# Moving the three operations of each unit that form the imaginary part of its second table from DVE to GpSimd

## What is computed

```
    lam_dt = lam * dt[:, None]
    lam_bar = jnp.exp(lam_dt)
    b_bar = ((lam_bar - 1.0) / lam)[..., None] * bmat
    powers = jnp.exp(lam_dt[None] * jnp.arange(1, S5_CHUNK + 1, ...)[:, None, None])
    ...
        _, xs = lax.associative_scan(_ssm_combine, (a, bu), axis=1)
        xs = xs + powers[None] * h[:, None]
        y = jnp.einsum('btgp,gsp->btgs', xs, cmat).real
```

## Time and profile before

| | |
|---|---|
| median of 3 runs | 1574.27 us (1570.85 to 1575.98) |
| span of the profiled execution, first to last instruction | 1571.2 us |
| PE busy | 1503.4 us, 96% |
| DVE busy | 872.9 us, 56% |
| ACT busy | 402.3 us, 26% |
| POOL busy | 565.2 us, 36% |
| share of PE in the chain that ended last | 88% |

### The profile page before, as it was taken

One profiled execution on the slowest core, in us unless ns is written; L12 is line 12 of the kernel. 1 busy time (PEld: TensorE's weight loads), 2 busy tenths in 40 slices (PEclk: granted clock), 3 DMA queues, 4 the chain that ended last, 5 costly groups with the idle time before them and its releaser, 6 DMA issues.

```text
span 1571.2 us, 25477 instructions
## 1 busy us (share of the span) xinstructions
PE 1503.4 (96%) x10192; PEld 1129.3 (72%) x10192; DVE 872.9 (56%) x1745; ACT 402.3 (26%) x956; POOL 565.2 (36%) x412
## 2 busy tenths in 40 slices
PE   4999989999999999999998999999999999999998
PEld 3455555666655558898877888887788874688887
DVE  5979944554578978378466321243543422265642
ACT  1222243333311222322233011001223550232210
POOL 4013340000002314101002977773496301477774
PEclk9999999999999999999999999999999999999999
DMA  9856771050286646747666455445544133455441
GB/s 332 221 173 194 242 237 45 3 159 14 100 262 228 202 174 180 273 166 287 251 252 260 159 195 182 161 163 185 191 167 146 70 108 107 131 179 164 168 150 68
DMA packets 172605, 272.99 MB, mean 174 GB/s; under 512 B 51405, under 2 KB 85304, under 8 KB 171208
## 3 DMA queue, kind: packets, MB, share of 16 engines
q1 hardware_dynamic: 146096, 201.08, 38.1%
q0 software_dynamic: 16512, 42.49, 8.4%
q10 hardware_dynamic: 9880, 27.78, 4.8%
HBM read 228.26 MB, written 42.99 MB: 173 GB/s over the span
## 4 chain that ended last, share of the span: by engine, by line
PE 88%; DVE 5%; DMA 3%; issue 2%; ACT 2%; POOL 0%; DVEq 0%; ACTq 0%; POOLq 0%
PE bank L499 82%; PE bank L502 6%; DMA memory<-in_w_mod 1%; DMA memory<-mc_scratch 1%; DVE memory L2417 1%; DVE memory L2418 1%; DVE memory L2424 0%; DVE memory L2421 0%; DMA memory<-in_s_log_dt 0%; DVE memory L2574 0%; ACT memory L1514 0%; ACT memory L1386 0%; ACT memory L1738 0%; DVE memory L2445 0%; DVE memory L2444 0%
## 5 line engine op out<-in xcount | busy, mean ns | idle before, releaser
L499 PE MATMUL bank<-memory 128*128 128x256 f32 (+8 forms) x9244 | 1404.7, 355 | 40.4 <-issue 8.5
L499 PEld LDWEIGHTS bank<-memory 128*128 128x128 f32 (+4 forms) x9244 | 1022.3, 166 | 378.1 <-issue 250.1
L2783 POOL DMA_DIRECT2D mc_scratch<-memory x32 | 28.0, 874 | 505.5 <-DVE memory L2138 447.7
L502 PEld LDWEIGHTS bank<-memory 128*128 128x128 f32 (+1 forms) x948 | 109.3, 142 | 59.4 <-issue 33.6
L502 PE MATMUL bank<-memory 128*128 128x128 f32 (+1 forms) x948 | 125.9, 277 | 23.5 <-ACT memory L1358 8.6
L2822 POOL TENSOR_TENSOR memory<-memory 128x1024 f32<-128x1024 f32 (+1 forms) x34 | 80.9, 2378 | 143.5 <-PE bank L499 96.2
L2808 POOL DMA_DIRECT2D memory<-mc_scratch x32 | 17.3, 541 | 189.7 <-PE bank L499 189.7
L2824 POOL TENSOR_TENSOR memory<-memory 128x1024 f32<-128x1024 f32 (+1 forms) x34 | 80.9, 2380 | 2.7
L2789 POOL DMA_DIRECT2D k_scratch<-memory x128 | 76.2, 629 | 14.5 <-ACT memory L1431 14.1
L2827 POOL TENSOR_TENSOR memory<-memory 128x1024 f32<-128x1024 f32 (+1 forms) x34 | 80.0, 2353 | 2.7
L2825 POOL TENSOR_TENSOR memory<-memory 128x1024 f32<-128x1024 f32 (+1 forms) x34 | 80.4, 2366 | 0.0
(11 more groups left out here) (305 smaller groups left out, 1284.3 us busy)
## 6 DMA issues: line engine op xcount, KB each, us to landing
memory<-in_s_w_glu SPq DMA_DIRECT2D x32, 1024.0 KB, 7.5
memory<-in_w_mod SPq DMA_DIRECT2D x12, 2048.0 KB, 14.1
memory<-in_w_ffn_up SPq DMA_DIRECT2D x22, 1024.0 KB, 6.9
memory<-in_w_in SPq DMA_DIRECT2D x10, 2048.0 KB, 8.0
mc_scratch<-memory POOLq DMA_DIRECT2D x32, 512.0 KB, 4.5
mb_scratch<-memory ACTq DMA_DIRECT2D x32, 512.0 KB, 3.7
memory<-mb_scratch SPq DMA_DIRECT2D x32, 512.0 KB, 7.3
memory<-mc_scratch POOLq DMA_DIRECT2D x32, 512.0 KB, 6.5
```

The source lines that it names most:

```text
L499: return nc.tensor.matmul(o, l, r, start=start, stop=stop, skip_group_check=free)
L502: return nc.tensor.transpose(o, i, ident[0:n, 0:n])
L2783: pool.dma_start(mc_dram[u], over(mc[:, u % 3, GS:GS + 1], (144, 8), (1, P))).then_inc(*S.up("mc_out%d" % (u % 3), u, by=16))
```

## The change

The three operations of the imaginary part (L2148, L2150, L2154) leave DVE. POOL gets them as a new function `imaginary_part(u)`, called for each unit ahead of `c_store(u)`, with a scratch `mb_part` of its own. The result has a signal of its own, `mb_im(u)`. PE's `unit_turned` waits for `mb(u)`, now the signal of the real part's sum, and for `mb_im(u)`. DVE waits once for `mb_im(31)`, before it overwrites the place where `mb_part` and the powers lie. DVE's remaining waits on its own earlier operations are renamed.

```diff
+        mb_part = take(512)
...
             def unit_turned(u):
 
                 pe.wait_ge(*S.at("mb", u))
+                pe.wait_ge(*S.at("mb_im", u))
...
                 tt(o[0], w[0], b[0], ALU.mult).then_inc(*S.up("unit_op", (u, 5)))
                 dve.wait_ge(*S.at("unit_op", (u, 4)))
-                tt(t[0], w[1], b[1], ALU.mult).then_inc(*S.up("unit_op", (u, 6)))
-                tt(o[1], w[0], b[1], ALU.mult).then_inc(*S.up("unit_op", (u, 7)))
-                dve.wait_ge(*S.at("mc", u))
-                tt(t[1], w[1], b[0], ALU.mult).then_inc(*S.up("unit_op", (u, 8)))
+                tt(t, w[1], b[1], ALU.mult).then_inc(*S.up("unit_op", (u, 6)))
                 dve.wait_ge(*S.at("unit_op", (u, 6)))
-                tt(o[0], o[0], t[0], ALU.subtract).then_inc(*S.up("unit_op", (u, 9)))
-                dve.wait_ge(*S.at("unit_op", (u, 8)))
-                tt(o[1], o[1], t[1], ALU.add).then_inc(*S.up("mb", u))
+                tt(o[0], o[0], t, ALU.subtract).then_inc(*S.up("mb", u))
...
+            dve.wait_ge(*S.at("mb_im", NU - 1))
             dve.wait_ge(*S.at("lnbc0"))
...
+            def imaginary_part(u):
+
+                b, w, o = mb_operands(u)
+                t = over(mb_part[:, 0:1], (P, 4), (GS, 8), (1, GS))
+                if u % 8 == 0:
+                    pool.wait_ge(*S.at("bbar", u // 8))
+                if u % 16 >= 2:
+                    pool.wait_ge(*S.at("mbT_mm", (u - 2, 1)))
+                if u == 16:
+                    pool.wait_ge(*S.at("bbd_zero", 1))
+                nc.gpsimd.tensor_tensor(o[1], w[0], b[1], ALU.mult).then_inc(*S.up("im_op", (u, 0)))
+                if u:
+                    pool.wait_ge(*S.at("mb_im", u - 1))
+                nc.gpsimd.tensor_tensor(t, w[1], b[0], ALU.mult).then_inc(*S.up("im_op", (u, 1)))
+                pool.wait_ge(*S.at("im_op", (u, 1)))
+                nc.gpsimd.tensor_tensor(o[1], o[1], t, ALU.add).then_inc(*S.up("mb_im", u))
...
             for half in range(2):
                 for u in range(16 * half, 16 * half + 16):
+                    imaginary_part(u)
                     c_store(u)
```

More of the change, by code:

```diff
@@ L258, in bbar_, with mb_operands @@
             return hT_flat[:, 3072:4096] if q == 2 else bbar[:, q % 2, :]
+        def mb_operands(u):
+            q, g8 = u // 8, u % 8
+            e = 288 * q + 9 * g8
+            b = [over(bbar_(q)[:, ri * 512 + g8 * GS:ri * 512 + g8 * GS + 1], (P, 4), (0, 8), (1, GS)) for ri in range(2)]
+            w = [over(pw[:, ri, e + 7:e + 8], (72, 4), (-1, 8), (0, GS)) for ri in range(2)]
+            o = [over(mb[:, u % 2, ri * P:ri * P + 1], (256, 4), (GS, 8), (1, GS)) for ri in range(2)]
+            return b, w, o
         def mbt_(u):
@@ L2128, in unit @@
                 if u:
-                    dve.wait_ge(*S.at("unit_op", (u - 1, 9)))
+                    dve.wait_ge(*S.at("mb", u - 1))
                 tt(t[0], w[1], c[1], ALU.mult).then_inc(*S.up("unit_op", (u, 1)))
@@ L2132, in unit @@
                 if u:
-                    dve.wait_ge(*S.at("mb", u - 1))
+                    dve.wait_ge(*S.at("mc", u - 1))
                 tt(t[1], w[1], c[0], ALU.mult).then_inc(*S.up("unit_op", (u, 3)))
@@ L2138, in unit @@
                 tt(o[1], o[1], t[1], ALU.subtract).then_inc(*S.up("mc", u))
[L2139 to L2142, removed]
+                b, w, o = mb_operands(u)
+                t = over(ut[:, 0:1], (P, 4), (GS, 8), (1, GS))
                 if u % 16 >= 2:
```

## The result

| | before | after |
|---|---|---|
| median of 4 runs each | 1573.57 us (1570.85 to 1575.98) | 1598.55 us (1596.12 to 1601.40) |
| ratio, 95% interval | | 1.0161 [1.0148, 1.0175] |
| span of the profiled execution | 1571.2 us | 1596.6 us |

The loss is 25 us (23 to 28 by the interval), where 17 were forecast. The direction, the place and the kind of loss were as predicted; the size was a third too small. What made it larger is for the most part how GpSimd's operations get their turns behind transfers, which no row of before could show, and most of the experiments are about it.

What follows compares the result with a forecast made beforehand. PE was taken to bound the kernel, with DVE just fast enough in the units. First stretch with unit 15, 8 us, plus 8.9 for units 16 to 27 gave 17 us: 1588 profiled, 1591 us median; range 1580 to 1630, the forecast's own 1580 to 1602.

Steps and rivals of the forecast that it cites:

- What bounds it: In both long stretches PE sets the time at 8.45 us a unit; DVE, at 7.63, is just fast enough.
- cover of 11 us for units 28 to 31: DVE's lead at unit 31 is 11 us; four units x 1.43 = 5.7 us against it cost nothing.
- the small operands don't collide: Rival, chance 0.08: DVE needs 5.82 us a unit, PE waits only at unit 15; 1572.5 us, no change.
- clean price: Where DVE and POOL alternate, a POOL operation costs DVE its length less 0.18 us: 1.08 for 512 columns.
- whole durations in turn: Rival, chance 0.11: short operations don't overlap, each POOL operation costs DVE 1.35 us; +36, 1611 us.
- a dearer POOL operation: Rival, chance 0.12: 16-column pieces slow POOL's operations to 1.80 us, 1630 us; at 2.35 us, 1670.
- faster: Rival, chance 0.05: no collision, and PE's clock stays up at unit 15, its wait 1.9 us; 1569.3 us.
- a unit's price on DVE: Each unit: three POOL operations cost DVE 3.24 us, 1.81 saved; 9.06 us instead of 7.63, 1.43 more.
- Slack, terms of the stretches: Units 3 to 14 and 16 to 27: 17.2 us each, less waits of 6.1 and 5.2, leads of 2.9 and 4.2.
- The 1.1 us for POOL's part of unit 27: In every odd unit POOL starts behind the taps and ends one operation after DVE, +1.1 us.
- The clock: PE's wait at unit 14 can lower its clock and lengthen transposes up to unit 15; counted as nothing, left to the bounds.
- The forecast signs: Trace signs: POOL operations 1.26 us alone, near 1.7 meeting DVE; DVE units 9 us apart; PE waits at units 14, 15, 23 to 27.

Runs made afterwards that it cites:

- two operations, fill and wait: Against the kernel with both products on GpSimd and the sum on DVE: one-element fill and wait for it ahead of each unit's first GpSimd operation; 1573.3 us, 0.9998.
- three, fill and wait: Against the changed kernel: GpSimd fills one element and waits for that fill ahead of each unit's first operation; 1580.0 us, 1.0043.
- kernels without collision: Against the changed kernel: GpSimd's three operations of a unit become fills with zeros, 1571.2 us; or GpSimd does none and DVE keeps nine, 1570.8 us.
- fills: Against the changed kernel: GpSimd's three operations of a unit become fills with zeros of 512, 896 and 896 columns, same places and waits; 1571.2 us, 0.9987.
- copies: Against the changed kernel: GpSimd's three operations of a unit become one-operand copies of 512 columns in the same places; 1571.8 us, 0.9984.
- floor kernel: Against the changed kernel: GpSimd's imaginary part, its signal and the waits for it go; DVE keeps nine operations of a unit; 1570.8 us, 0.9987.

## Why the prediction was right, and where not

**What bounds it: right.** PE's pace of 8.45 us against DVE's decided: at 8.3 us (two operations, fill and wait) there is no loss, at 8.8 (three, fill and wait) there is. The cover of 11 us for units 28 to 31 held: unit 31 is as late as unit 27.

**The sign and the mechanism: right.** DVE and GpSimd exclude each other. The rival "the small operands don't collide" falls with the held operations, and its price of 1572.5 us is about what the kernels without collision gave (1571.2 and 1570.8). The clean price, an operation's length less 0.18 us, which I read from operations of 2.35 us, holds for short ones: 0.87 for 1.05 us, 1.08 for 1.27, 0.42 for a copy of 0.62. The rival "whole durations in turn" falls with this, "a dearer POOL operation" with the lengths alone (1.05 to 1.27 us), and "faster" with the held operations.

The Trainium skill, page "SBUF — State Buffer", section "Who interferes with whom", says that a DVE instruction with two inputs there contends with a GpSimd instruction that reads there and not with one that only writes. The trace agrees: 0 held operations beside fills, 84 beside copies.

**What was mis-sized: a unit's price on DVE (1.08 for each operation, 3.24 held for 1.81 saved).** Three things in it are off, not all in one direction. The two products take 1.05 to 1.09 us alone, not 1.26; only the sum takes 1.27. Clean turns are therefore 0.87 + 0.87 + 1.08 = 2.82 us a unit, 24 x 0.42 = 10 us less than forecast in the 24 units of the two stretches. The nine operations left take 5.95 us, not 5.82, which adds 3. And the turns are not all clean: DVE's operations are held by 80.2 us in these units, where 24 x 2.82 would be 67.7. Of the 12.5 between them the eight early holds make 7; the rest comes from the eleven double turns, each 0.5 to 1 us above two clean turns.

So a unit was held by 3.34 us on average, next to my 3.24, but for other reasons: two misses of 10 and 12.5 us all but cancelled, and that the forecast came out as near as it did is in part luck. The sum of the three is some 39 us more of DVE's time in the 24 units, where 24 x 1.43 = 34 were forecast. That is 5 of the 8 us by which the loss of the profiled execution, 25.4, exceeds my 17.

The kernel with fill and wait on all units is the check on the clean price. My sum with 2.82 and 5.95 is 17 - 10 + 3 = 10 us; it measured 6.8. Its DVE is held by 58.0 us in the 24 units and not by 67.7, mostly because 7 of GpSimd's 72 operations there fall beside other work of DVE or before its unit begins. This is also why the wait gave back 18.6 us, more than the 12.5 of early holds and double turns.

**Slack, terms of the stretches: right in kind.** Waits of 6.1 and 5.2 us and leads of 2.9 and 4.2 were to be used up first, and they were. The measured delay is 8.8 us at unit 14 (7.1 forecast), 2.0 more at unit 15 (1 forecast), 13.0 in units 16 to 27 (8.9 forecast) and 1.5 behind 660 us (nothing forecast). What the dearer units don't explain of this is 1.0 at unit 15, the 1.5 at the end, and 1 us in smaller terms. The 1.1 us for POOL's part of unit 27 ending behind DVE's did not come: it ends at 582.9 us, DVE's at 586.4. And of the 3.1 us between span and median, 1.9 is the step from a span to its time (1596.6 and 1598.5 in the profiled run after).

**The clock: counted as nothing, and that was nearly right.** The granted clock was 0.98 in both stretches (1.00 before), up to 2 us of PE's time in each. But PE waits for DVE's last operation at units 14 and 27 (4.17 and 1.89 us in the rows above), and DVE is busy for 105.36 of 106.00 us: DVE sets the time there, and a faster PE would have waited longer. This is part of why PE's waits for units rose by only 22.3 - 3.7 = 18.6 us and the span by 25.4. Behind unit 14 DVE waits for PE's transposes before it can begin unit 15; the lower clock there can have added 1.0 us at most:

```profile
216.00:220.00 4.00, 3.65 (x24) 3.28 (x23) 1.78 (x3) 2.06 (x4) 3.98 (x6) 0.74 0.83 234
```

Behind unit 15 it is 0.50 from 227 to 231 us and 0.90 from 231 to 235, no worse than 0.50 and 0.70.

**The forecast signs.** GpSimd's operations, 1.26 us alone and near 1.7 where they meet DVE: the sum does (1265 to 1687 ns), the products run at 1.05 and 1.6. Some three of nine DVE operations at 1.7 to 1.8 us, in units 9 us apart: none to six of a unit are held, most of them at 1.5 to 1.8 us and the longest at 3.46, and many units alternate, 11.9 and 7.0 us for 25 and 26; on average a unit takes 9.2 and 9.4 us of DVE's time in the two stretches. PE's waits, 7 us at unit 14, 4 to 6 at unit 15 and 9 behind: 4.2 at unit 14 with 3.5 at units 9 and 11 before it, 4.9, and 9.8 from unit 23 on. The waits stand behind DVE, as said, not behind GpSimd's queue.

**Not settled.** The 1.5 us behind 660 us: PE's waits for `mc_scratch` between 700 and 960 us are 3.5 us there and 0.7 before, but no run was made on them. Why a reading operation behind transfers holds DVE before it is recorded. And which engine gets the next turn: in the kernel with one product on GpSimd this product began 0.24 and 0.23 us behind the start of a DVE operation in units 10 and 12; it got the next turn in the one (1.43 us) and waited for ten DVE operations in the other (7.18 us).

## What to carry to other kernels

Moving work from DVE to GpSimd frees DVE only if it saves more than GpSimd's reading operations take: price each at its length alone less 0.2 us, for DVE operations with two operands in memory, and compare DVE's new pace with the engine that consumes its results. Put nothing that reads memory directly behind transfers in GpSimd's queue, or put a wait between them that can end only when the transfers have been issued; here a fill and a wait for it were worth 18.6 of 25 us. And take the operation's length alone from a row of its own kind: products and sums of the same size differed by 0.2 us.

## What the runs showed of the hardware that was not expected

- A GpSimd operation queued behind its own transfers held a DVE operation by 0.87 us, from before it was recorded as begun (558.33 to 559.95 against 559.73), and then held the next again; this happened in eight of the 24 units of the two stretches. A wait for a fill ahead of it ended this (25 us of loss fell to 6.8); the fill alone did not (26).
- GpSimd can take two turns in a row (2.93 us on DVE for two operations of 1.12), and DVE ten (7.18 us on GpSimd for an operation that takes 1.05 alone).
- A copy with one operand excludes DVE as well (0.42 us); a fill does not.
- After a wait of PE of 2.04 to 2.05 us for unit 15 the granted clock stayed at 1.00 in the floor kernel; over 4 us behind it, it was 0.57 with only unit 15 on GpSimd, 0.57 with copies and 0.62 with fills.
